# Attention norm, LayerNorm and 72 convolution taps moved into the branch merge of a diffusion trunk, the merge in order of branches, late modulation chunks in four buffers

## What is computed

```python
mod = silu(cvec) @ w_ada + b_ada                  # 6 chunks of 1024: sh1, sc1, g1, sh2, sc2, g2
h = rms_norm(x, rms1_g) * (1 + sc1) + sh1
q, k, v, up, uc = split(h @ w_in)
o = diff_attention(rope(rms_norm(q)), rope(rms_norm(k)), v, lam)    # 8 heads
o = rms_norm(o, subln_g) * (1.0 - lam_init)
y_a = o @ w_proj_a
y_b = multiscale_pool(up) @ w_proj_b
z = a * sigmoid(b)                                # a, b: the two halves of uc, 512 channels
z = depthwise_conv(z, conv_w, width 31) + conv_b
y_c = silu(layer_norm(z, ln_g, ln_b)) @ w_proj_c
ga, gb, gc = split(sigmoid(h @ w_gate + b_gate))
x = x + g1 * ((ga * y_a + gb * y_b + gc * y_c) @ w_out)
x = x + g2 * expert_choice_ffn(rms_norm(x, rms2_g) * (1 + sc2) + sh2)   # 16 experts
```

## Time and profile before

| | us |
|---|---|
| three runs: median (lowest to highest) | 3322.55 (3313.8 to 3324.69) |
| the profiled execution: its time | 3326.58 |
| the profiled execution: span of the trace | 3324.5 |
| PE busy | 2942.1 (88%) |
| DVE busy | 1978.3 (60%) |
| ACT busy | 1460.9 (44%) |
| POOL busy | 459.5 (14%) |

### The profile page before, as it was taken

One profiled execution on the slowest core, in us unless ns is written; L12 is line 12 of the kernel. 1 busy time (PEld: TensorE's weight loads), 2 busy tenths in 40 slices (PEclk: granted clock), 3 DMA queues, 4 the chain that ended last, 5 costly groups with the idle time before them and its releaser, 6 DMA issues.

```text
span 3324.5 us, 42592 instructions
## 1 busy us (share of the span) xinstructions
PE 2942.1 (88%) x16896; PEld 2267.9 (68%) x16896; DVE 1978.3 (60%) x1880; ACT 1460.9 (44%) x1588; POOL 459.5 (14%) x259
## 2 busy tenths in 40 slices
PE   5979887999985999999859798879999859999997
PEld 4978764887883666666549787648878836666664
DVE  3198874211135888888632988742111358888885
ACT  4135553211124677777442355432111246777774
POOL 0321110000001122122203211100000011222122
PEclk8989998999997999999979999889999979999998
DMA  6211124212125999999832111242222259999994
GB/s 239 69 55 45 45 72 169 77 64 64 64 89 187 335 367 380 370 367 379 305 124 58 53 45 45 96 146 77 64 64 64 89 202 335 375 374 369 373 373 165
DMA packets 238382, 601.12 MB, mean 181 GB/s; under 512 B 13536, under 2 KB 116096, under 8 KB 237472
## 3 DMA queue, kind: packets, MB, share of 16 engines
q1 hardware_dynamic: 224896, 549.09, 45.4%
q0 software_dynamic: 10272, 34.26, 4.0%
q10 hardware_dynamic: 3072, 15.73, 1.2%
HBM read 570.72 MB, written 28.31 MB: 180 GB/s over the span
## 4 chain that ended last, share of the span: by engine, by line
PE 78%; DVE 11%; DMA 5%; ACT 2%; issue 2%; SPq 1%; POOL 0%; DVEq 0%; ACTq 0%; POOLq 0%; PEldq 0%
PE ps L1254 19%; PE ps L1255 19%; PE ps L1256 19%; PE ps L1292 8%; DVE zc L941 4%; DMA raw<-in_w_ada 2%; PE ps L1417 2%; PE ps L1393 1%; DMA xg<-h_dram,next_token 1%; PE ps L1567 1%; PE ps L1406 1%; DMA raw<-in_w_in 1%; PE ps L1337 1%; DVE w_lo L850 1%; DVE stats L971 1%
## 5 line engine op out<-in xcount | busy, mean ns | idle before, releaser
L1254 PE MATMUL ps<-h_hi,w_hi 128*128 128x320 f32 x1408 | 448.3, 318 | 81.1 <-DVE h_lo L899 48.0
L1169 DVE TENSOR_TENSOR m_lo<-m_raw_b,m_hi 128x2048 fp32r<-128x2048 f32 x192 | 439.4, 2289 | 73.4 <-ACT m_hi L794 71.6
L1169 DVE TENSOR_TENSOR m_lo<-m_raw_a,m_hi 128x2048 fp32r<-128x2048 f32 x192 | 438.8, 2288 | 69.7 <-ACT m_hi L794 67.7
L794 ACT CAST m_hi<-m_raw_b 128x2048 fp32r<-128x2048 f32 x192 | 367.1, 1912 | 179.0 <-PE ps L1256 179.0
L1255 PE MATMUL ps<-h_lo,w_hi 128*128 128x320 f32 x1408 | 441.2, 313 | 0.0
L1256 PE MATMUL ps<-h_hi,w_lo 128*128 128x320 f32 x1408 | 440.8, 313 | 0.0
L794 ACT CAST m_hi<-m_raw_a 128x2048 fp32r<-128x2048 f32 x192 | 366.4, 1911 | 164.6 <-PE ps L1256 161.5
L1254 PE MATMUL ps<-m_hi,xs_hi 128*80 128x512 f32 x1024 | 409.1, 400 | 3.3 <-DVE xs_lo L1184 3.3
L1255 PE MATMUL ps<-m_lo,xs_hi 128*80 128x512 f32 x1024 | 406.4, 397 | 0.0
L1256 PE MATMUL ps<-m_hi,xs_lo 128*80 128x512 f32 x1024 | 404.4, 395 | 0.0
L500 ACT CAST w_hi<-raw 128x2048 fp32r<-128x2048 f32 x68 | 129.2, 1902 | 552.4 <-DMA raw<-in_w_gate 335.7
(11 more groups left out here) (257 smaller groups left out, 4744.7 us busy)
## 6 DMA issues: line engine op xcount, KB each, us to landing
m_raw_a<-in_w SPq DMA_DIRECT2D x192, 1024.0 KB, 7.4
m_raw_b<-in_w SPq DMA_DIRECT2D x192, 1024.0 KB, 7.4
raw<-in_w_in SPq DMA_DIRECT2D x72, 512.0 KB, 4.7
raw<-in_w_ada SPq DMA_DIRECT2D x64, 512.0 KB, 4.7
raw<-in_w_gate SPq DMA_DIRECT2D x48, 512.0 KB, 6.2
m_raw_a<-in_w_ada SPq DMA_DIRECT2D x8, 1024.0 KB, 9.6
m_raw_b<-in_w_ada SPq DMA_DIRECT2D x8, 1024.0 KB, 15.6
raw<-in_w_proj_a SPq DMA_DIRECT2D x16, 512.0 KB, 4.1
```

The lines of the kernel that those rows point to most:

```text
L794: nc.scalar.copy(m_hi[:, n % RING], m_raw(slot)).then_inc(s["m_high"], 1)
L1169: nc.vector.tensor_tensor(m_lo[:, r], m_raw(slot), m_hi[:, r].bitcast(F32), ALU.subtract).then_inc(s["msplit"], 1)
L1254: pe.matmul(out, wh, xh, start=first, stop=False, skip_group_check=True)
```

## The change

The convolution's taps are dealt out anew: 24 ahead of the first unit, 6 in each of the first three pairs, 10 in the last, 72 in the first six steps of the merge. The merge runs by branch: four steps of pooling, four of attention, four of convolution, unrolled. The separate norm stage is gone; PE issues its products between the quarters of gate products: the sums over the heads' squares (`o_sums`) in step 0, the broadcast of the inverse roots (`o_rows`) in steps 1 and 2, the two LayerNorm sums (`ln_sums`) in steps 6 and 7, all in banks 4 to 7. The squares of `o` go to the space of `x`, so `x` comes back from DRAM in step 3 (it did in the second step before). The 16 late modulation chunks go through four buffers: the two `raw` and, once all tiles are done, the unused second halves of the split buffers. The product of gate and projection is written over the sigmoid's tile.

```diff
-MERGE = [(q, b) for q in range(2) for b in (1, 0, 2)]
+MERGE = [(n, b) for b in (1, 0, 2) for n in range(4)]
...
+        osq = sb("o_squares", [P, HEADS, TOK], r_x)
+        ada_raw_a = sb("ada_raw_a", [P, EK, FF], r_ring + 49152)
+        ada_raw_b = sb("ada_raw_b", [P, EK, FF], r_ring + 65536)
...
```

SP, the late modulation chunks and the merge's weights:

```diff
                 for i in range(2 * RAWS):
-                    u = 1 - i % 2
-                    chunk(u, (two[:, 0], src[:, 0]), (two[:, 1], src[:, 1]))
+                    u = i % 4
+                    if u < 2:
+                        chunk(1 - u, (two[:, 0], src[:, 0]), (two[:, 1], src[:, 1]))
+                    else:
+                        if i < 4:
+                            sp.wait_ge(s["qkv"], 36 * (l + 1))
+                        else:
+                            sp.wait_ge(s[f"ada_free{u}"], 4 * l + i // 4)
+                        sp.dma_start((ada_raw_a, ada_raw_b)[u - 2][:], src).then_inc(s[f"ada_full{u}"], 16)
+                for i, (n, b) in enumerate(MERGE):
...
+                    if i == 3:
+                        sp.wait_ge(s["o_var"], l + 1)
+                        sp.dma_start(x[:].rearrange("p k n -> p (k n)"), x_dram).then_inc(s["x_back"], 16)
...
```

DVE, the taps ahead of the first unit and in the units of a pair:

```diff
-                conv(8)
+                conv(6)
                 sums_of(0)
                 conv(2)
...
-                conv(8)
+                conv(6)
                 sums_of(1)
...
-                conv(16)
+                conv(8)
...
                             if i == 0:
-                                conv(4)
+                                conv(1)
                             if i == 1:
-                                conv(2)
                                 split_low((3 * n + 1) % 2, 0)
                             if i in (2, 5):
-                                conv(4)
+                                conv(1)
...
```

DVE, the merge:

```diff
+                for i, (n, b) in enumerate(MERGE):
+                    split_low((i + 1) % 2, 0)
+                    if i == 0:
+                        conv(5)
+                        o_variance()
+                        conv(5)
+                        o_inverse()
+                    if i in (1, 2):
+                        o_scale(4 * i - 4, 4 * i)
+                    if 1 <= i <= 5:
+                        conv((10, 10, 12, 15, 15)[i - 1])
+                    if i == 5:
+                        dve.sem_inc(s["conv_done"], 1)
+                    if i == 6:
+                        ln_center()
+                    if i == 7:
+                        ln_scale()
+                    dve.wait_ge(s["sig"], seen("sig"))
+                    dve.wait_ge(s["proj"], seen("proj", 2))
+                    if b == 1:
+                        nc.vector.tensor_tensor(merged4[:, n], ps[:, 4:8, 0:HALF], sigd[:], ALU.mult).then_inc(s["merged"], 1)
+                        dve.wait_ge(s["merged"], seen("merged") + 1)
+                        dve.sem_inc(s["set_free1"], 1)
+                    else:
+                        link(nc.vector.tensor_tensor(sigd[:], ps[:, 4:8, 0:HALF], sigd[:], ALU.mult))
+                        dve.sem_inc(s["set_free1"], 1)
+                        nc.vector.tensor_tensor(merged4[:, n], merged4[:, n], sigd[:], ALU.add).then_inc(s["merged"], 1)
...
```

PE, the broadcast of two heads' roots and the merge:

```diff
+                def o_rows(first):
+                    if first == 0:
+                        pe.wait_ge(s["o_inv"], seen("o_inv"))
+                    if first % 4 == 0:
+                        wait_set(1)
+                    else:
+                        pe.wait_ge(s["o_norm"], HEADS * l + first)
+                    for h in (first, first + 1):
+                        b = 4 + 2 * (h % 2)
+                        for c, (a, e) in enumerate(halves):
+                            ins = pe.matmul(ps[:, b + c, 0:HALF], ident[0:HEADS, h:h + 1].to_broadcast([HEADS, P]), row[0:HEADS, a:e], start=True, stop=True)
+                        ins.then_inc(s["o_ss"], 1)
...
+                for i, (n, b) in enumerate(MERGE):
+                    def between(j, c):
+                        if i and (j, c) == (0, 1):
+                            release((i + 1) % 2)
+                        if i == 0 and (j, c) == (1, 0):
+                            o_sums()
+                        if i in (1, 2) and c == 1:
+                            o_rows(4 * i - 4 + 2 * j)
+                        if i == 6 and (j, c) == (1, 0):
+                            pe.wait_ge(s["conv_done"], l + 1)
+                            ln_sums(4, lambda g: (zc[:, g, 0:LAT], zc[:, g, LAT + CPAD:CRUN]), None)
+                        if i == 7 and (j, c) == (1, 0):
+                            ln_sums(6, lambda g: (brc[:, g, 0:LAT], brc[:, g, LAT:TOK]), "ln_sq")
+                    wait_split(i % 2)
+                    wait_set(0)
+                    feature_split(i % 2, 0, halves, between)
...
+                    feature_raw(1, 1, halves, src, kt)
```

More of the change, by code:

```diff
@@ L739, in _ @@
[L739 to L754 removed]
+                    nc.scalar.activation(osq[:, h], ot[:, h], ACT.Square).then_inc(s["o_sq"], 1)
@@ new lines, in o_roots, with ln_squares @@
+                def o_roots():
+                    act.wait_ge(s["sum0_t"], seen("sum0_t"))
+                    nc.scalar.activation(row2[0:HEADS], flat[0:HEADS, 6 * 512:6 * 512 + TOK], ACT.Square, scale=EPS ** 0.5).then_inc(s["sum0_sq"], 1)
+                    act.wait_ge(s["o_var"], seen("o_var"))
+                    nc.scalar.activation(row[0:HEADS], row[0:HEADS], ACT.Sqrt).then_inc(s["o_sqrt"], 1)
+                def ln_squares():
+                    act.wait_ge(s["ln_d"], seen("ln_d"))
+                    for j in range(GROUPS):
+                        nc.scalar.activation(brc[:, j, 0:LAT], zc[:, j, 0:LAT], ACT.Square)
+                        nc.scalar.activation(brc[:, j, LAT:TOK], zc[:, j, LAT + CPAD:CRUN], ACT.Square).then_inc(s["ln_sq"], 1)
@@ new lines, in ln_root, with ln_silu @@
+                def ln_root():
+                    act.wait_ge(s["ln_var"], seen("ln_var"))
+                    nc.scalar.activation(row2[:], row2[:], ACT.Sqrt).then_inc(s["ln_sqrt"], 1)
+                def ln_silu():
+                    act.wait_ge(s["ln_n"], seen("ln_n"))
+                    for j in range(GROUPS):
+                        for a, b, z in ((0, LAT, 0), (LAT, TOK, CPAD)):
+                            ins = nc.scalar.activation(brc[:, j, a:b], zc[:, j, a + z:b + z], ACT.Silu,
+                                                       scale=small_at("ln_g")[:, j:j + 1], bias=small_at("ln_b")[:, j:j + 1])
+                        ins.then_inc(s["branch_c"], 1)
@@ new lines, in _ @@
+                for i, (n, b) in enumerate(MERGE):
+                    split_high((i + 1) % 2, 0)
+                    skip_raw(1)
+                    if i == 0:
+                        o_roots()
+                    if i == 7:
+                        ln_root()
+                    act.wait_ge(s["proj"], seen("proj"))
+                    act.wait_ge(s["merged"], seen("merged"))
+                    for j in range(2):
+                        at = SMALL["b_gate"][0] + 8 * b + 2 * n + j
+                        for h in range(2):
+                            ins = nc.scalar.activation(sigd[:, 2 * j + h], ps[:, 2 * j + h, 0:HALF], ACT.Sigmoid, bias=sm[:, at:at + 1])
+                    ins.then_inc(s["sig"], 1)
+                    act.wait_ge(s["sig"], seen("sig"))
+                    act.sem_inc(s["set_free0"], 1)
+                    seen("proj")
+                    if i == 6:
+                        ln_squares()
+                    if i == 7:
+                        ln_silu()
@@ L1070, in _ @@
[L1070 to L1087 removed]
+                    dve.wait_ge(s["sum0_sq"], seen("sum0_sq"))
@@ new lines, in ln_sums @@
+                def ln_sums(bank, src, sem):
+                    wait_set(1)
+                    for j in range(GROUPS):
+                        if sem:
+                            pe.wait_ge(s[sem], seen(sem))
+                        lat, own = src(j)
+                        pe.matmul(ps[:, bank, :], ones[:], lat, start=(j == 0), stop=(j == GROUPS - 1), skip_group_check=True)
+                        ins = pe.matmul(ps[:, bank + 1, 0:CTX], ones[:], own, start=(j == 0), stop=(j == GROUPS - 1), skip_group_check=True)
+                    ins.then_inc(s["ln_sum"], 1)
```

273 lines of the change are left out of this document (108 added, 165 removed).

## The result

| | kernel before | changed kernel |
|---|---|---|
| median | 3323.62 us (4 runs, 3313.8 to 3325.32) | 3196.46 us (4 runs, 3193.35 to 3200.91) |
| profiled execution | 3326.6 us, span 3324.5 | 3193.35 us, span 3191.5 |
| mean granted clock | 0.942 | 0.959 |

The ratio is 0.9624, with an interval of 0.9602 to 0.9647: 127 us less.

What follows compares the result with a forecast made beforehand. The prediction took PE, busy for 88% of the span, as the bound, with gains from its idle or slow time. Its terms, 55 + 24 + 27 = 106 us, gave a median of 3216.5 us, range 3175 to 3260.

Steps and rivals of the forecast that it cites:

- Terms 1 and 2: Attention pairs 0 to 2: moving taps off DVE removes PE's waits for it, 27 + 28 = 55 us.
- term 1: First unit of attention: with 12 fewer taps ahead, maximum starts 8.6 us sooner, 4.9 more follow; 13.5 us a layer.
- Term 3: Late modulation in the last pair: four buffers remove all of PE's waits for `w_ada` chunks, 24 us.
- Term 4: Norms and merge: norm products move between gate products, 364 us become 350.3, gaining 13.7 a layer, 27 us.
- its stall: Merge steps 1 and 2: PE waits for scaled heads, then runs slow; 8.3 us a step, 16.6 for two.
- The clock stays up and the wait is short: Merge broadcasts: 8-row products do not lower the clock, 3197 us; with DVE's low half early too, 3183; chance 0.19.
- The late taps: Merge: taps cost 2.15 us each and hold steps up, 39 us in all, giving 3255; chance 0.15.
- the waits on ACT in place of DVE's: Attention: waits return on ACT's exponentials and copies, 26 us less gain, giving 3242; chance 0.08.
- the merge at 1.2 GHz: Merge: gate products between broadcasts, sums and waits never regain the clock, 153 us lost a layer, giving 3522; chance 0.04.

Runs made afterwards that it cites:

- the yardstick: The changed kernel run once more without any edit, beside later runs on the same chip: 3197.07 us, ratio 0.9622 to the kernel before.
- the run with the early scaling: The changed kernel with the first two heads of merge steps 1 and 2 scaled ahead of the weights' low half on DVE: 3183.46 us, ratio 0.9586.

## Why the prediction was right or wrong

| term | forecast | measured |
|---|---|---|
| 12 taps ahead of the first unit | 2 x 8.6 = 17 | 16 |
| the other taps of pairs 0 to 2 | 2 x 4.9 + 28 = 38 | 53 - 16 = 37 |
| late modulation, four buffers | 24 | 24 to 25 |
| norms and merge | 27 | 44 between the traces |

- **Terms 1 and 2 held, in size and cause.** Within term 1 two errors cancelled. "The scores themselves come some 1.8 us sooner" was wrong: DVE's norm of the second head came 0.9 us sooner (205.69 against 206.56), but the first scores started at 215.05, against 214.70 before, and PE's products ahead of them were no sooner either (the first of the transposes ahead of them started at 209.34, against 208.98). The maximum followed the scores at once, as forecast, but 6.25 us sooner than before and not 8.6. Unit 1 to unit 2 then gained 7.0 us in place of 4.9, so the two parts make 13.2 in layer 0 where 13.5 was forecast; that the sum fits so well is luck.
- **Term 3 held.** All of the waits went, none on ACT took their place: a unit of the last pair takes some 5.7 us, and PE is busy for 40.1 of the 42 us from 461 to 503. The transfers came near to being the bound: there the DMA engines moved 337 GB/s at a busy share of 0.93, so more buffers would give little.
- **Term 4 is the step that failed, by its stall.** The prediction said "A step then loses 3.5 + 2.2 + 2.6 = 8.3, two 16.6." The steps 1 and 2 took 31.86 and 33.32 us in layer 0, 30.30 and 30.84 in layer 1, where their products take 22.7 + 2 x 2.4 = 27.5: 10.1 and 6.1 us in place of 16.6 and 16.6, or 17 us less for the two layers, and 27 + 17 is the 44 measured. The wait was timed well for DVE (heads ready 15.9 us into the step, forecast 16.3), but PE came at 13.5 rather than 12.8, so 2.49 and not 3.5. The 2.2 us for a second broadcast at 1.2 GHz were wrong in the main: it takes 2.4 us at 1.00 in three of the four steps, and 3.00 at 0.79 in the fourth (in the yardstick's profile one took 4.6 at 0.50). What slows down more are the full products behind it. And wait and slow products are not added, as I did: a slow stretch ahead of the second broadcast uses up the wait (7.31 + 2.49 = 9.80 in step 1, 8.83 + 0.87 = 9.70 in step 2). Two smaller things partly cancel: step 0 starts at 0.50 behind the last values (9.5 and 8.1 us for two quarters, 7.3 at full clock), and norms and merge took 365.9 and 366.9 us before, where I had taken 364.
- **What the loop is worth stood in the sum without a line of its own.** "This leaves out the turn of the loop" hid 318 - 306.7 = 11.3 us a layer, 22.6 in all; the run says 20. The norms moved inside were left with 46 - 43.6 = 2.4 us a layer, and gained 5 by the runs (10 in two layers), 7 by the traces. A reader of the prediction would have taken the 27 us for the norms; most of them were the loop's.
- **The rivals.** "The clock stays up and the wait is short" gave 3197, which is the measured time, but its mechanism is half wrong: the broadcasts do run at full clock where no wait stands ahead of them, and the waits are shorter, but the products behind the broadcasts pay. That its number fits is luck: it takes 19 us out of the stall, and 17 came out, in another way. The late taps did not come (no wait on them in any step, and the merge as long without them), nor the waits on ACT in place of DVE's, nor the merge at 1.2 GHz; the clock fell only for some 5 us behind a broadcast, and in some broadcasts behind a wait.
- **The rule of the Trainium skill** (TensorE: Matmul & The Clock Gate, Part 1: The HAM clock gate), by which activity opens the gate and idling shuts it, was right on the broadcasts themselves where no wait stands ahead of them, and there I went against it. It does not give what the run with the early scaling shows, 0.67 to 0.83 behind a broadcast with PE busy throughout, and not the block of 17.56 us at 0.50 that 128 rows bring to 1.00.
- **What stays open.** The single edits add up to 53 + 24 + 10 + 20 = 107 us of 127, and each of the four ratios is uncertain by 7 to 13 us. The stages in the traces leave less open. From the last values to the end of the merge, two layers together, writing out the loop gained 21.6 us, the new form of the norm stage 4.4, the order by branches 1.4, moving the norms inside 15.4 (the 14 from above, counted from the last values), and the rest of the change 1.6: 44, which is all that this stage gained. With 54 for the taps in pairs 0 to 2 and 28 for the buffers in the last pair, from the traces with each undone, that is 126, where the stages that the change touches gained 124.3. Whether some of the 8.7 us outside them comes from the change is not shown. Why a quarter behind a broadcast of 8 rows is sometimes spared stays open too.

## What to carry to other kernels

When a side engine has work without a deadline, look for the stage in which the main engine is full and the side engine idle, and count taps per unit, not in total: the first one lies under another engine's work, only those behind it are waited for. Before crediting a rearrangement, price what is undone on the way, such as a loop that has to be written out; here it was 20 us, and could be had alone. And of a TensorE block with few rows of weights look at the clock of what stands behind it; filling the rows with zeros cost nothing on PE here (1.91 us a block in place of 2.35).

## What the runs showed of the hardware that was not expected

- Blocks of broadcasts of 8 weight rows with no wait ahead ran at a granted clock of 1.00 in 2.35 us, and 21 of 32 were followed by 24 full products at 0.67 without any gap (5.2 us in place of 3.6); with 128 rows none of 28 was. Why 11 were spared was not tried.
- The same number of broadcasts over 128 rows took 1.91 us a block in place of 2.35, so the zeros did not make them longer.
- With 128 rows a gap of 1.93 us was followed by 3.7 us at 0.54 and then by 1.00, and one of 2.41 us by 1.00 throughout.
- The turn of a loop of two, on PE, showed as two gaps of 5.34 and 2.47 us with no other engine named, then 5.6 us at a clock of 0.50; it cost 10.7 us in layer 0 and 10.9 in layer 1. What in the turn takes this time, no trace shows.
